# Who clears the Toeplitz table, and where four value tiles stand, in the state-space part of a two-block kernel

## The chip, the cores and the metric

The kernel runs on one core of a Trainium2 chip. The metric is the device time of one execution in microseconds. A core has TensorE (matmuls), VectorE, ScalarE, GpSimd, and SyncE, which here issues all DMAs. Each engine works through its own instructions in order and waits on semaphores. TensorE writes to PSUM, eight banks of 128 x 512 float32.

## The reference

Two transformer blocks over x of 1 x 1024 x 1024, all float32. The first block mixes a state-space part (S5) and retention, then a convolutional feed-forward; the second has three branches (differential attention, and two gated linear attentions), then a feed-forward. The change is in the first block's mixer:

```
h = x @ w_in                        # 1024 -> 512 (u), 256 (q), 256 (k), 512 (v), 512 (gate)
bu = einsum('blgc,gpc->blgp', u, b_bar)                   # 32 groups, 64 complex states
_, states = associative_scan(_ssm_combine, (a_elems, bu))
y = real(einsum('blgp,gcp->blgc', states, c)) + d * u
y = gelu(y);  y_s5 = rms_norm(y * sigmoid(y @ glu_w + glu_b))
y_ret = retention(rotary(q), rotary(k), v) * silu(gate)   # 16 chunks of 64, 4 heads
x = layer_norm(ALPHA * x + concat(y_s5, y_ret) @ w_out)
```

## The kernel before

Every float32 weight is cut in two parts, high and low, and each product is made of three matmuls (high x high, high x low, low x high). A weight unit of 128 x 1024 is loaded into one of three buffers WR, ScalarE writes its high part WH (L1167), GpSimd its low part WL (L2538), and there are five places for cut units. `act_cut(e, done)` and `pool_cut(e, done)` run up to five units ahead of `done`. Units 0 to 3 are the state-space input, 4 to 7 the queries and keys, 8 to 11 the values, 12 and 13 the weights of the gated linear unit (GLU).

The order of the work is written out by hand on each engine. The PSUM banks are handed out by a counter in the order of TensorE's program (`claim`), so an instruction moved there also moves the banks of what follows: a claim waits until the last user of its bank has been read.

**The state-space part** works in eight positions of a block at a time. With TensorE it computes: `kernel_of(p)`, four groups of the short convolution kernel (L548); `inject(q)`, eight groups that bring the input into the states (L537); `outputs(q)`, four groups of 32 T8 products (L561) with twice as many products of the states (L563). In its words a value tile is one step of `values` (`tick(values, n)`), 24 matmuls of 128 x 512 (L476 to L478) that make one of eight tiles of v. It has nothing to do with the state-space part and fills TensorE's time in it.

T8 is the Toeplitz table, 128 x 32 x 128, 16 KB on each partition. It is zero above its diagonal blocks. GpSimd adds the diagonal term to the four parts of the kernel (`through`, L2649), clears T8 (L2673), and SyncE, which waits for the clearing (`s_t8z`), writes the eight shifted copies of the kernel from memory into it (L2846). T8 lies over the tables from which the kernel was made, so it can be cleared only when these have been read (`s_et`, `s_kd`). `outputs(0)` waits for T8 (`t8_in`) and for the states of its group (`s_ss`).

VectorE turns each injected group by the phase table ET, scans it along the time and turns it back (`dve_s5`); it waits for `inject(q)` and frees that group's bank with the fifth of its instructions (L1910). After each second group it reports four more groups of states (`s_ss`).

ScalarE copies the value tiles from PSUM into the buffer STQ (L1198), from where SyncE spills them to memory, and applies gelu to the outputs (L1220, L1222), which needs another function table than the copies. Behind the state-space part comes retention: SyncE loads the spilled queries and keys back (QKC) when all states are done, GpSimd rotates them (L2626 to L2637), TensorE transposes them (`flip`, L502) and computes the scores (`scores`, L604), with value tiles 5, 6 and 7 in between. ScalarE copies the transposed chunks (KQT, L1172), and between two of them cuts the landed state-space output YP for the GLU (GH, L1335).

Of the kernel before, what the change touches and what calls it, by code (L numbers as in the profile page):

```python
# [10 lines left out]
ACT = mybir.ActivationFunctionType  # L11
# [238 lines left out]
def build(nc, D, out):  # L250
    plan, order1, order2 = weight_plan()
    with ExitStack() as ctx:
# [3 lines left out]
        def sem(name):  # L256
# [19 lines left out]
        s_pp, s_cl, s_bb, s_et, s_t8z, s_kd, s_ss = (sem(n) for n in (  # L276
            "s5_powers", "s5_c_powers", "s5_b_powers", "s5_tables_read", "s5_toeplitz_zero", "s5_kernel_done", "s5_states"))
# [40 lines left out]
        ones = sb("ones", 204.5, [128, 128])  # L318
# [38 lines left out]
        T8 = sb("T8", 132, [128, 32, 128])  # L357
# [57 lines left out]
        lots = bk.at  # L415
# [89 lines left out]
        def pe_mixer(e):  # L505
            prep = claim(e, "prep", 2, hold=True, told=False)
            for p in range(4):
                v = wt.next("w_in", 0, 8, 128 * p, 128)
                u = claim(e, ("u", p), 2)
# [64 lines left out]
            values = pe_token_steps(e, "v", "w_in", 1024, 0, 8, XH, XL, range(8))  # L574
# [9 lines left out]
            tick(values, 2)  # L584
            inject(4)
            inject(5)
            outputs(0)
            tick(values, 1)
            inject(6)
            inject(7)  # L590
            outputs(1)
            tick(values, 1)
            outputs(2)
            tick(values, 1)
            outputs(3)

            def scores(i):
# [304 lines left out]
        def tick(steps, n):  # L902
            for _ in range(n):
                next(steps, None)
# [296 lines left out]
        def act_s5(e):  # L1201
            def turned(q):
                act_evac(e, lots["bbt", q], BB[:, 2 * q:2 * q + 2, :, :].rearrange("p a b c -> p (a b c)"))

            def kernel_of(p):
                u = lots["kt", p]
                k = KTS[p % 2]
                if p == 1:
                    e.wait_ge(s_cl, 4)
                if p >= 2:  # L1210
                    e.wait_ge(kt_out[p % 2], 16)
                e.wait_ge(u.full, u.nfull)
                e.activation(k[:, 0:8:2, :], PS[0:16, u.b, :].rearrange("p (a c) -> p a c", a=4), ACT.Copy).then_inc(act, ca.up())
                e.activation(k[:, 1:8:2, :], PS[0:16, u.b + 1, :].rearrange("p (a c) -> p a c", a=4),
                             ACT.Copy).then_inc(u.drained, 1)

            def outputs(q):
                u = lots["y8", q]
                e.wait_ge(u.full, u.nfull)
                e.activation(U8[:, 8 * q:8 * q + 8:2, :], PS[:, u.b, :].rearrange("p (a c) -> p a c", a=4),  # L1220
                             ACT.Gelu_apprx_tanh).then_inc(act, ca.up())
                e.activation(U8[:, 8 * q + 1:8 * q + 8:2, :], PS[:, u.b + 1, :].rearrange("p (a c) -> p a c", a=4),  # L1222
                             ACT.Gelu_apprx_tanh).then_inc(u.drained, 1)

            def values(*blocks):
                for i in blocks:
                    act_spill(e, "v", i)

            for i in range(5):
                act_spill(e, "qk", i)  # L1230
            for q in range(4):
                turned(q)
            act_spill(e, "qk", 5)
            act_spill(e, "qk", 6)
            for q in range(4, 8):
                turned(q)
            act_spill(e, "qk", 7, 4)
            kernel_of(0)
            kernel_of(1)
            act_cut(e, 6)  # L1240
            kernel_of(2)
            kernel_of(3)
            act_cut(e, lots["qk", 7].units)
            values(0, 1)
            outputs(0)
            values(2)
            outputs(1)
            values(3)
            outputs(2)
            values(4)  # L1250
            outputs(3)

        def act_retention(e):
# [1387 lines left out]
        def pool_kernel(e):  # L2641
            idb = ident[0:16, 0:16].rearrange("p (o c) -> p o c", o=1).to_broadcast([16, 8, 16])
            e.wait_ge(dm_in, 16)
            e.wait_ge(cst, 32)

            def through(p):
                u, k = lots["kt", p], KTS[p % 2]
                e.wait_ge(u.drained, u.ndrained)
                e.tensor_tensor(k[:, :, 0:16], k[:, :, 0:16], diag(p), ALU.add).then_inc(s_kd, 1)  # L2649

            def diag(p):
                return sm[0:16, 128 * (p % 2):128 * (p % 2) + 128].rearrange("p (g c) -> p g c", c=16)

            def spread(p):
                if p >= 2:
                    e.wait_ge(s_kd, p - 1)
                e.tensor_tensor(diag(p), idb, DM[:, 8 * p:8 * p + 8].rearrange("p (g o) -> p g o", o=1).to_broadcast([16, 8, 16]),
                                ALU.mult).then_inc(pool, cg.up())
                e.wait_ge(pool, cg.n)

            spread(0)
            spread(1)
            through(0)
            through(1)
            spread(2)
            spread(3)
            pool_cut(e, 6)
            through(2)
            through(3)
            u = lots["kt", 3]  # L2670
            e.wait_ge(u.full, u.nfull)
            e.wait_ge(s_et, 1)
            e.memset(T8[:, :, :], 0.0).then_inc(s_t8z, 1)  # L2673
            pool_cut(e, lots["qk", 7].units)

        def cuts(cut, e, name):
# [526 lines left out]
```

## Time and profile before

| | us |
|---|---|
| median of three runs (3144.47 to 3147.0) | 3144.47 |
| the profiled execution | 3141.87 |
| its span, first to last instruction | 3139.6 |
| TensorE busy in it | 3041.6 (97%) |
| ScalarE, VectorE, GpSimd busy | 913.7, 1245.6, 1047.0 |

The granted TensorE clock is 0.991 of full speed in the mean over the span. The stretch of the change is 100 to 215 us; the kernel goes on for another 2900 us after it. A timeline row gives start, duration, engine, line, operation, written tile and read tiles, and in brackets the idle time before it and what ended it. Rows of several instructions are merged (x4). In the profile T8 is called T, U8 is U, and M1 to M3 are M.

### The profile page before, as it was taken

To read this page: it belongs to the slowest core of one execution; us is meant where nothing else is said; L and a number is where in the kernel's file an instruction comes from. 1 tells how busy PE (TensorE), PEld (TensorE's weight loads), DVE (VectorE), ACT (ScalarE), POOL (GpSimd) and SP (SyncE) were. 2 spreads that over 40 slices of the span, in tenths; PEclk is the share of its full clock that TensorE was granted. 3 is DMA by queue.
4 is the path that set the end of the run, shared out by engine and by line. 5 is a ranking of instruction groups with operands and counts; after the bars stand their busy time and mean duration, and the time that the engine had idled before them with its cause. 6 is when DMAs were issued, how large, how long until landed. Compare 5 with 4: busy or idle time off the path is not lost.

```text
span 3139.6 us, 35710 instructions
## 1 busy us (share of the span) xinstructions
PE 3041.6 (97%) x14710; PEld 2499.1 (80%) x14710; DVE 1245.6 (40%) x2353; ACT 913.7 (29%) x1340; POOL 1047.0 (33%) x514
## 2 busy tenths in 40 slices
PE   8999999999999999999999999999999999999998
PEld 7777788888888877777777777788888788888886
DVE  8837642112221155454536644532545111121115
ACT  3223342121211233333424543432333212111111
POOL 4443354322323252111322333232223733333335
PEclk9899999999999999999999999999999999999999
DMA  6332311111111112111110111124330111111111
GB/s 210 85 110 69 101 47 48 53 62 47 47 47 54 47 63 88 48 55 61 41 44 31 54 47 54 41 68 157 138 134 28 59 49 68 47 47 47 54 41 54
DMA packets 70897, 207.62 MB, mean 66 GB/s; under 512 B 11376, under 2 KB 19968, under 8 KB 70720
## 3 DMA queue, kind: packets, MB, share of 16 engines
q1 hardware_dynamic: 70736, 205.34, 20.4%
q8 instruction: 117, 1.92, 0.3%
q14 instruction: 44, 0.36, 0.0%
HBM read 172.54 MB, written 32.77 MB: 65 GB/s over the span
## 4 chain that ended last, share of the span: by engine, by line
PE 85%; POOL 4%; ACT 3%; DVE 3%; issue 3%; DMA 1%; SPq 0%; ACTq 0%; DVEq 0%; POOLq 0%
PE PS L436 48%; PE PS L476 7%; PE PS L478 7%; PE PS L477 7%; PE PS L756 3%; PE PS L1067 3%; POOL WL L2538 2%; PE PS L944 1%; PE PS L974 1%; PE PS L502 1%; PE PS L563 1%; PE PS L858 1%; PE PS L859 1%; PE PS L857 1%; PE PS L957 1%
## 5 line engine op out<-in xcount | busy, mean ns | idle before, releaser
L2538 POOL TENSOR_TENSOR WL<-WR,WH 128x1024 fp32r<-128x1024 f32 x241 | 580.5, 2416 | 1853.9 <-ACT WH L1167 1853.8
L436 PE MATMUL PS<-XH,WH 128*128 128x512 f32 x2176 | 690.8, 399 | 16.9 <-DVE XL L1788 9.2
L436 PE MATMUL PS<-XL,WH 128*128 128x512 f32 x2176 | 674.4, 391 | 0.0
L436 PE MATMUL PS<-XH,WL 128*128 128x512 f32 x2176 | 672.2, 390 | 0.0
L436 PEld LDWEIGHTS PS<-XH,WH 128*128 128x128 f32 x2176 | 397.1, 189 | 108.4 <-issue 25.4
L436 PEld LDWEIGHTS PS<-XL,WH 128*128 128x128 f32 x2176 | 410.1, 188 | 87.4
L436 PEld LDWEIGHTS PS<-XH,WL 128*128 128x128 f32 x2176 | 409.6, 188 | 87.7
L1167 ACT ACTIVATE WH<-WR 128x1024 fp32r<-128x1024 f32 x241 | 253.2, 1055 | 666.8 <-PE PS L478 443.3
L476 PE MATMUL PS<-WH,HH 128*128 128x512 f32 x736 | 286.4, 389 | 2.5 <-POOL HL L2570 2.5
L477 PE MATMUL PS<-WL,HH 128*128 128x512 f32 x736 | 286.3, 389 | 0.0
L478 PE MATMUL PS<-WH,HL 128*128 128x512 f32 x736 | 286.3, 389 | 0.0
L2167 DVE TENSOR_TENSOR CT<-CT,PS 128x1024 f32<-128x1024 f32 x54 | 65.9, 1221 | 459.1 <-ACT CT L1392 310.9
L2180 DVE TENSOR_TENSOR XF<-XF,PS 128x512 f32<-128x512 f32 x160 | 110.0, 687 | 313.2 <-PE PS L478 313.2
L476 PEld LDWEIGHTS PS<-WH,HH 128*128 128x128 f32 x736 | 138.1, 188 | 31.6 <-POOL HL L2570 2.9
L478 PEld LDWEIGHTS PS<-WH,HL 128*128 128x128 f32 x736 | 138.1, 188 | 28.7
L477 PEld LDWEIGHTS PS<-WL,HH 128*128 128x128 f32 x736 | 138.1, 188 | 28.7
L476 PE MATMUL PS<-WH,XH 128*128 128x512 f32 x384 | 153.7, 400 | 4.7 <-POOL WL L2538 3.0
L478 PE MATMUL PS<-WH,XL 128*128 128x512 f32 x384 | 151.4, 394 | 0.0
L477 PE MATMUL PS<-WL,XH 128*128 128x512 f32 x384 | 151.2, 394 | 0.0
L2570 POOL TENSOR_TENSOR HL<-CT,HH 128x1024 fp32r<-128x1024 f32 x54 | 129.5, 2399 | 7.6 <-ACT HH L1398 7.6
L2161 DVE SCALAR_TENSOR_TENSOR CT<-PS,cols,CT 128x1023 f32<-128x1023 f32 x22 | 28.2, 1283 | 238.3 <-ACT CT L1385 238.3
L2389 DVE COPY_PREDICATED ST<-LV,PS 128x512 f32<-128x512 uint8 x128 | 85.7, 726 | 70.0 <-PE PS L1067 69.8
(349 smaller groups left out, 3986.0 us busy)
## 6 DMA issues: line engine op xcount, KB each, us to landing
WR<-in_weights SPq DMA_DIRECT2D x241, 512.0 KB, 3.6
gates<-EG SPq DMA_DIRECT2D x18, 512.0 KB, 5.2
EI<-gates SPq DMA_DIRECT2D x18, 512.0 KB, 4.7
BR<-brbuf SPq DMA_DIRECT2D x12, 512.0 KB, 6.3
RAWX<-in_xT SPq DMA_DIRECT2D x8, 512.0 KB, 7.6
spill<-STQ SPq DMA_DIRECT2D x16, 256.0 KB, 2.3
RX<-in_x SPq DMA_DIRECT2D x8, 512.0 KB, 6.5
xbuf<-XF SPq DMA_DIRECT2D x8, 512.0 KB, 2.6
```

Source lines behind the costliest of these rows:

```text
L436: last = e.matmul(PS[:, u.b + h, :], w, x[:, k, 512 * h:512 * h + 512], start=k == 0 and w is w1 and x is xh, stop=k == nk - 1 and w is w2)
L476: e.matmul(PS[:, u.b, :], a, wh[:, k, :], start=j == 0 and k == 0, stop=False)
L477: e.matmul(PS[:, u.b, :], a, wl[:, k, :], start=False, stop=False)
L478: last = e.matmul(PS[:, u.b, :], c, wh[:, k, :], start=False, stop=j == len(vs) - 1 and k == 1)
L756: last = e.matmul(PS[:, u.b + h, :], w[:, k, :], x[:, k, 512 * h:512 * h + 512], start=k == 0 and w is wh and x is XH, stop=k == 7 and w i ...
L1067: last = e.matmul(PS[:, us[g][hh].b, 128 * (i % 4):128 * (i % 4) + 128], kl[rows[hh], c], kr[rows[hh], c], start=True, stop=True)
L1167: e.activation(WH[:, v % NSPL, :], WR[:, v % NRAW, :], ACT.Copy).then_inc(w_hi, 1)
L2167: e.tensor_tensor(X, X, bank(u, 2), ALU.mult).then_inc(u.drained, 1)
L2180: e.tensor_tensor(x, x, bank(u), ALU.add).then_inc(u.drained, 1)
L2389: e.copy_predicated(o, LV[:, n:n + 1, :].to_broadcast([128, 4, 128]), four(u)).then_inc(u.drained, 1)
L2538: e.tensor_tensor(WL[:, v % NSPL, :], WR[:, v % NRAW, :], WH[:, v % NSPL, :].bitcast(F), ALU.subtract).then_inc(w_lo, 1)
L2570: e.tensor_tensor(HL[:, v % 5, :], CT[:, v % 2, :], HH[:, v % 5, :].bitcast(F), ALU.subtract).then_inc(f_lo, 1)
```

## The change

Four edits, all of them in order alone; no arithmetic is added or removed:

- ScalarE clears T8, with a copy of the ones table scaled by 0, behind its cuts of units 11 and 12 and ahead of value tile 0. It waits for `s_et` and for all four kernel parts (`s_kd`).
- GpSimd no longer clears it, so that the low parts of units 11 and 12 stand right behind the last two kernel additions.
- On TensorE value tiles 2 and 3 stand ahead of `outputs(0)`; tile 4 stands behind `outputs(1)`. Before, tile 2 stood behind `outputs(0)`, tile 3 behind `outputs(1)`, tile 4 behind `outputs(2)`.
- ScalarE's copies follow: tiles 0 to 3, then the gelu of two output groups, tile 4, the gelu of the last two.

SyncE's program is the same: it still stores output group 0 ahead of value tile 2 and group 1 ahead of tile 3.

```diff
@@ pe_mixer @@
             inject(4)
             inject(5)
+            tick(values, 2)
             outputs(0)
-            tick(values, 1)
             inject(6)
             inject(7)
             outputs(1)
             tick(values, 1)
             outputs(2)
-            tick(values, 1)
             outputs(3)
@@ act_s5 @@
             act_cut(e, lots["qk", 7].units)
-            values(0, 1)
+            e.wait_ge(s_et, 1)
+            e.wait_ge(s_kd, 4)
+            e.activation(T8[:, :, :], ones[:, :].rearrange("p (o c) -> p o c", o=1).to_broadcast([128, 32, 128]), ACT.Copy,
+                         scale=0.0).then_inc(s_t8z, 1)
+            values(0, 1, 2, 3)
             outputs(0)
-            values(2)
             outputs(1)
-            values(3)
+            values(4)
             outputs(2)
-            values(4)
             outputs(3)
@@ pool_kernel @@
             through(3)
-            u = lots["kt", 3]
-            e.wait_ge(u.full, u.nfull)
-            e.wait_ge(s_et, 1)
-            e.memset(T8[:, :, :], 0.0).then_inc(s_t8z, 1)
             pool_cut(e, lots["qk", 7].units)
```

TensorE, from value tile 1's end to output group 1, before. L537 is an injected group, L561 an output group's first product, L476 the first matmul of a value tile; rows without a wait are left out.

```order
L537 MATMUL PS<-U_71,BB 64x128 [waits bank0_drained,bank4_drained]
...
L561 MATMUL PS<-U_71,T_116 128x128 [waits t8_landed,s5_states,bank2_drained]
...
L476 MATMUL PS<-WH,XH 128x512 [waits bank4_drained]
...
L537 MATMUL PS<-U_71,BB 64x128 [waits bank5_drained]
...
L537 MATMUL PS<-U_71,BB 64x128 [waits bank6_drained]
...
L561 MATMUL PS<-U_71,T_116 128x128 [waits s5_states,bank1_drained,bank0_drained]
```

The same place now:

```order
L537 MATMUL PS<-U_71,BB 64x128 [waits bank0_drained,bank4_drained]
...
L476 MATMUL PS<-WH,XH 128x512 [waits bank2_drained]
...
L561 MATMUL PS<-U_71,T_116 128x128 [waits s5_states,t8_landed,bank5_drained,bank4_drained]
...
L537 MATMUL PS<-U_71,BB 64x128 [waits bank6_drained,bank5_drained]
...
L537 MATMUL PS<-U_71,BB 64x128 [waits bank7_drained,bank6_drained]
...
L561 MATMUL PS<-U_71,T_116 128x128 [waits s5_states,bank1_drained,bank0_drained]
```

Two value tiles (each begins with a wait for bank 2 or a neighbour) have moved ahead of output group 0, and that group now takes banks 4 and 5, which were injected groups 2 and 3's, instead of 2 and 3.

GpSimd, from the last two kernel additions to the first rotated chunk, before:

```order
L2649 TENSOR_TENSOR KTS_107<-KTS_107,sm 16x8x16 [waits bank0_drained]
L2649 TENSOR_TENSOR KTS_108<-KTS_108,sm 16x8x16 [waits bank2_drained]
L2673 MEMSET T_116 128x4096 [waits s5_tables_read,bank2_full]
L2538 TENSOR_TENSOR WL<-WR,WH 128x1024 [waits weight_high_cut] x2
L2626 TENSOR_TENSOR TA_81<-QKC,RT 128x256 [waits ret_tables_landed,qk_chunk_landed0]
```

The same place now:

```order
L2650 TENSOR_TENSOR KTS_107<-KTS_107,sm 16x8x16 [waits bank0_drained]
L2650 TENSOR_TENSOR KTS_108<-KTS_108,sm 16x8x16 [waits bank2_drained]
L2539 TENSOR_TENSOR WL<-WR,WH 128x1024 [waits weight_high_cut] x2
L2627 TENSOR_TENSOR TA_81<-QKC,RT 128x256 [waits ret_tables_landed,qk_chunk_landed0]
```

The clearing is gone, and the two low parts have nothing ahead of them but the additions.

## Rows read from the trace of the kernel before

**Rows 1.** Chain of waits, 100 to 215 us: start us, us, what.
```profile
113.62 3.48 POOL T L2673
...
122.23 9.14 DMA T<-ktbuf
...
192.33 0.65 PE PS L563 x4
```

**Rows 2.** Windows, TensorE: stretch, us, busy (instructions), granted clock, DMA share, GB/s.
```profile
116.40:119.40 3.00, 0.32 (x2) 1.00 0.13 14
...
131.50:146.50 15.00, 14.99 (x49) 0.50 0.31 121
...
146.50:151.70 5.20, 5.20 (x13) 0.50 0.46 75
```

**Rows 3.** Timeline, TensorE: start us, us, line, operation [idle before, releaser].
```profile
119.44 0.50 PE L476 MATMUL PS<-WH,XH 128*128 128x512 f32 x1 [2.73 <-POOL WL L2538]
...
131.51 0.76 PE L561 MATMUL PS<-U,T 128*128 128x128 f32 x2 [3.07 <-DMA T<-ktbuf]
...
146.46 0.79 PE L476 MATMUL PS<-WH,XH 128*128 128x512 f32 x1
...
154.71 1.97 PE L537 MATMUL PS<-U,BB 128*64 128x128 f32 x32
...
156.60 0.49 PE L561 MATMUL PS<-U,T 128*128 128x128 f32 x2
...
165.06 0.50 PE L476 MATMUL PS<-WH,XH 128*128 128x512 f32 x1
...
170.63 0.38 PE L561 MATMUL PS<-U,T 128*128 128x128 f32 x2
```

**Rows 4.** Timeline, GpSimd (POOL), 85 to 262 us.
```profile
107.69 4.85 POOL L2538 TENSOR_TENSOR WL<-WR,WH 128x1024 fp32r<-128x1024 f32 x2
...
113.57 3.52 POOL L2673 MEMSET T<- 128x4096 f32 x1
...
117.06 4.67 POOL L2538 TENSOR_TENSOR WL<-WR,WH 128x1024 fp32r<-128x1024 f32 x2
...
176.72 0.72 POOL L2626 TENSOR_TENSOR TA<-QKC,RT 128x256 f32<-128x256 f32 x1 [54.99 <-DMA QKC<-spill]
...
186.47 0.61 POOL L2637 TENSOR_TENSOR KZ<-QKC,RT 128x256 f32<-128x256 f32 x1
```

**Rows 5.** Timeline, VectorE (DVE), 85 to 262 us.
```profile
108.18 2.15 DVE L1749 TENSOR_TENSOR BB<-M 128x256 f32<-128x256 f32 x1
...
110.36 4.01 DVE L1749 TENSOR_TENSOR_SCAN BB<-LAM,BB 128x128 f32<-128x128 f32 x4
...
115.26 0.42 DVE L1749 TENSOR_TENSOR BB<-M 128x256 f32<-128x256 f32 x1
...
116.51 5.51 DVE L1749 TENSOR_TENSOR BB<-M 128x256 f32<-128x256 f32 x1
...
122.05 1.80 DVE L1749 TENSOR_TENSOR_SCAN BB<-LAM,BB 128x128 f32<-128x128 f32 x4
...
147.56 0.42 DVE L1749 TENSOR_TENSOR BB<-M 128x256 f32<-128x256 f32 x1
...
155.90 0.42 DVE L1749 TENSOR_TENSOR M<-PS,ET 128x256 f32<-128x256 f32 x1 [1.87 <-PE PS L537]
...
168.14 0.69 DVE L1931 TENSOR_TENSOR BB<-M,M 128x508 f32<-128x508 f32 x1
```

**Rows 6.** Timeline, ScalarE (ACT), 85 to 262 us.
```profile
113.90 1.06 ACT L1167 ACTIVATE WH<-WR 128x1024 fp32r<-128x1024 f32 x1 [1.26 <-DMA WR<-in_weights]
...
121.19 0.60 ACT L1198 ACTIVATE STQ<-PS 128x512 f32<-128x512 f32 x1 [6.23 <-PE PS L478]
...
204.95 1.06 ACT L1335 ACTIVATE GH<-YP 128x1024 fp32r<-128x1024 f32 x1 [1.05 <-DMA YP<-ybuf]
...
205.92 0.58 ACT L1172 ACTIVATE KQT<-PS 128x512 f32<-128x512 f32 x1
```

## Prediction

> **What bounds the kernel now.** I read the busy line first: TensorE is busy 97% of the span, so only its idle time and its clock can give anything. Then I followed the chain of waits through the stretch that the diff touches, 100 to 215 us. It goes: GpSimd's last kernel addition, the clearing of T8 (3.48 us from 113.62), eight Toeplitz loads, the landing of the last of them after 9.14 us at 131.37, and from there only TensorE's own work until the last output group ends at 192.98 [rows 1]. The reader is to see that the chain runs through the clearing, not through TensorE's work before 131.37: two value tiles and the state matmuls end at 128.44 and then TensorE waits 3.07 us [rows 3].
>
> The granted clock is the second thing to see. It is 1.00 (the 2.4 GHz level) in the wait at 116.4 and 0.50 (1.2 GHz) from 131.5 to 151.7, right behind the second wait [rows 2]. Output group 0 takes 14.95 us there (131.51 to 146.46), group 1 at the full clock 8.46 (156.60 to 165.06). Value tile 2 takes 8.25 (146.46 to 154.71), tile 3 at the full clock 5.57 (165.06 to 170.63) [rows 3]. So the wait of 3.07 costs 9.2 us more in slow matmuls than it lasts itself.
>
> A third, smaller loss: value tile 0 stands 2.73 us for the low part of weight unit 11, which GpSimd makes only behind the clearing, at 117.06 [rows 3, 4].
>
> **The change, part by part.** Times are those of the trace of before, moved.
>
> Clearing on ScalarE. Its last cut before the value tiles ends at 114.96 [rows 6]. Its copies take 0.60 us for 512 columns and 1.06 for 1024 [rows 6], 0.9 ns a column, so 4096 columns cost some 3.8 us (bounds: 3.5, as GpSimd's clearing, and 7.6, twice the price of a column, which no plain copy in the rows comes near). The table is clear at 118.8 instead of 117.10, and SyncE's eight loads, the two weight loads and the tables behind them go out 1.7 us later. T8 lands at 133.1 instead of 131.37. Behind the clearing on ScalarE stand the copies of value tiles 0 to 3; tile 0 ends near 117.8, so its copy waits 1 us, on no path, since the PSUM bank is not wanted again soon. Even the upper bound lands T8 at 136.9.
>
> Two value tiles before output group 0. By the sum below TensorE comes to group 0 at 139.2. T8 is there 6 us before that. The 3.07 us are gone, and with them the only idle time that stood ahead of the fall of the clock: gain 3.07 + (14.95 - 8.46) + (8.25 - 5.57) = 3.07 + 6.49 + 2.68 = **12.2 us**. Value tile 4 moves to between groups 1 and 2: no work added or removed.
>
> GpSimd's low parts follow each other. Unit 11's can start at 113.6 and end near 116.0, before tile 0 wants it at 116.4: the 2.73 us are gone at that place. But what is late next? Tile 1 goes to bank 7, which VectorE frees when it has read state group 1 out of PSUM. Before, it had done so at 116.47 (the instruction ahead of the one at 116.51), in the shadow of the clearing, and its instructions with two SBUF inputs ran at full pace in that time (0.42 us at 115.26) [rows 5]. Beside low parts they don't: the subtraction at 108.18 took 2.15 us and the four scans 4.01 instead of 1.80 while GpSimd made two low parts from 107.69, and the subtraction at 116.51 took 5.51, until the pair from 117.06 was through at 121.73 [rows 4, 5]. Now the pair runs 113.6 to 118.4 and falls on the fourth scan. If VectorE slips in between the two parts (as at 110.33), group 1 is read by 120.2; if not (as at 116.51), by 121.0. Before, tile 1 began at 119.44 plus a quarter of a tile, 120.8. So this part gives between +0.6 and -0.2; I take **0.2 us**, not 2.7.
>
> The Trainium skill, page "SBUF — State Buffer", section "Who interferes with whom", says that a VectorE instruction with two SBUF inputs and a GpSimd instruction that reads SBUF exclude each other for the whole instruction; a clearing reads nothing. By that rule the moved low parts do hit the scan, and the edit's own gain is the 0.2 above; without it tile 1 would begin at 117.8 and the sum would be 15. The trace agrees (0.42 against 5.51 us).
>
> VectorE from there: its next scans began at 122.05; now at 120.7 to 121.5, so its chain runs 0.5 to 1.4 us earlier, and its wait of 1.87 us for state group 6 goes too, since TensorE does that group at 147.7. Its last states come at 168.83 - 1 - 1.87 = 166.0 [rows 5].
>
> The banks move with the tiles. Output group 0 now takes the banks of state groups 2 and 3, group 1 those of 4 and 5. Group 5 was read just ahead of the instruction at 147.56 [rows 5], now by 147; output group 1 starts at 149.6. That is a margin of over 2 us and costs nothing.
>
> Sum for TensorE: tile 1 from 120.6 to 126.05; state groups 4, 5 to 128.2; tiles 2, 3 to 139.2; output 0 to 147.7; states 6, 7 to 149.6; output 1 to 158.1; tile 4 to 163.6; outputs 2 and 3 to 180.5. Before: 192.98. That is **12.4 us**.
>
> Retention's start. The rotated keys need VectorE's last states (166.0) and then the load. GpSimd began on them at 176.72, 7.9 us after the states, and was through with two chunks at 187.08 [rows 4]. In front of that load SyncE stores output group 1 and a value tile; group 1 ends at 158.1 now, and the stores are gone by 163 (an estimate), so the states set the load, the keys begin between 171 and 174 and two chunks are done by 181 to 184. The first transpose needs one chunk at 180.5, the second both, more than 6 us later. New waits: scores 0 takes the bank of tile 5 and stands for its copy (0.60 us), tile 6 stands for the masking of scores 0, tile 7 for the copy of the second transposed chunk. That copy ended at 206.50, 13.5 us after the last output group, since it stands in ScalarE's queue behind the landing of YP's last quarter [rows 6]; tile 7 is wanted two tiles (11.1) and an estimated 2.5 us of small work and the two waits after it, 13.6. Against that tile 5 no longer stands for a copy. I take 0, between -1 and +1. Behind that the free banks are those of two places earlier throughout, which changes who waits for whom only around two of the six gated jobs: under 1 us either way.
>
> **Sum: 12.4 us, taken as 12.5.** The profiled execution took 3141.87 us (span 3139.6), so 3129.4 on its basis; it is the fastest of those shown. On the median, 3144.47, it is **3132.0**.
>
> **Rivals.**
> - No collision on VectorE. For it: a scan's second input is one column repeated. Against: the scans at 110.36. Tile 1 starts 2.8 us earlier: 15.3 us, 3129.2. 10%.
> - The clock halves once anyway. TensorE still stands 2.4 to 3.2 us before tile 1 and has the thin matmuls of the states before and behind. Against: the wait of 2.73 at the same place left the clock at 1.00 [rows 2]. Same price as before, 9.2 us: gain 3.3, 3141.2, which a measurement can't tell from no change (I take 0.2%, 6.3 us, as what it can tell). 11%.
> - Retention takes it back: tile 7 stands for the chunk's copy. The margin is nil, and YP's landing waits in SyncE's queue behind sixteen small stores and three loads. Each us late is lost; with 4 us 3136.0. 9%.
> - Slower. The clock halves at the wait before tile 1 and stays there past the 20.2 us that it lasted before. A tile costs 4.9 us more then (12 in 5.2 us at the half clock, beside the one begun before [rows 2], so 24 in 10.4), so tiles 1 to 3 eat 14.7 us, more than the gain: from the third tile on it is a loss. With output group 0 (6.5) it is 21.2 - 12.5 = 8.7 slower, 3153.2. Against it: a busy TensorE had its clock back after 20 us. 4%.
>
> **How the numbers follow.** Forecast 66%, rivals 10, 11, 9 and 4. The forecast's own range is 3129.5 to 3134.5 (bounds of the collision and of retention's start). From 3126.5 (first rival, and a run as much below the median as the profiled one) to 3141.5 (second rival) all but the slow case and some tails are inside. Faster by over 0.2%: the forecast, the first rival and most of the third, 84%. Within 0.2%: 12%. Slower: 4%.
>
> **What would show it.** Granted clock 1.00 from 120 to 180; no wait of TensorE for T8; output group 0 in 8.5 us beginning near 139; a wait of some 2.4 to 3.2 us before value tile 1 where there was one of 2.73 inside tile 0; a scan of VectorE stretched over GpSimd's pair; ScalarE's clearing 3.5 to 4.2 us; the last output group's end near 180.5; tile 7 without a long wait. It is wrong if a stretch of 0.50 stands behind 120, if output group 0 still ends with T8's landing, or if the 12 us at 180 are no longer there at 215.

## The result, and the profile after

The changed kernel takes 3133.36 us in the median of six executions (3127.94 to 3136.61), the kernel before 3144.47 of six (3140.63 to 3147.0). The ratio is 0.9966, with a 95% interval of 0.9955 to 0.9976: 11.1 us faster. Nine more executions, measured later beside fourteen of the kernel before, gave a median of 3135.7 against 3144.11, ratio 0.9976 (0.9967 to 0.9986): 8.4 us faster. The profiled execution took 3131.03 us, its span is 3129.2 at a mean granted clock of 0.994 (before: 3139.6 at 0.991). Three executions of all that follow (one of before, 3419 us; one each of two experiments, 7861 and 9967 us) were slow as a whole and are left out.

Places are compared from one landmark on: GpSimd's last two kernel additions, at 112.51 us before and at 113.78 after, because the two spans don't begin alike. Line numbers of after are one more or one less than before.

TensorE's timeline, after, answers to [rows 3] (start, duration, engine, line, operation, written tile and read tiles; in brackets the idle time before it and what ended it):

```profile
122.86 0.50 PE L476 MATMUL PS<-WH,XH 128*128 128x512 f32 x1 [3.52 <-DVE M L1911]
...
130.12 1.97 PE L537 MATMUL PS<-U,BB 128*64 128x128 f32 x32
132.01 0.50 PE L476 MATMUL PS<-WH,XH 128*128 128x512 f32 x1
...
143.03 0.38 PE L561 MATMUL PS<-U,T 128*128 128x128 f32 x2
...
151.37 1.97 PE L537 MATMUL PS<-U,BB 128*64 128x128 f32 x32
184.14 0.66 PE L502 MATMUL PS<-ident,QKC 128*128 128x128 f32 x4
...
191.12 0.71 PE L603 MATMUL PS<-KQT 64*128 64x128 f32 x8 [0.84 <-ACT STQ L1197]
192.68 0.50 PE L476 MATMUL PS<-WH,XH 128*128 128x512 f32 x1 [0.26 <-DVE PT L1952]
...
214.52 0.70 PE L436 MATMUL PS<-GH,WH 128*128 128x512 f32 x2 [1.30 <-ACT SG L1260]
```

The wait for T8 is gone. Output group 0 runs from 143.03 to 151.37, 8.3 us instead of 14.95; tiles 2 and 3 together take the 11.0 us from 132.01. Tile 0 no longer stops, but tile 1 now begins with a wait of 3.52 us, for the bank that VectorE reads.

The windows view of TensorE, after, answers to [rows 2] (window, length, busy time and matmuls, granted clock, DMA share, GB/s):

```profile
119.40:122.80 3.40, 0.00 (x0) 1.00 0.24 33
122.90:124.10 1.20, 1.20 (x5) 1.00 0.96 170
124.20:127.40 3.20, 3.20 (x9) 0.50 1.32 121
127.80:130.10 2.30, 2.30 (x11) 1.00 1.87 189
132.10:143.00 10.90, 10.90 (x48) 1.00 0.56 200
```

After the wait the clock is at its full 2.4 GHz for 1.3 us, then at 1.2 GHz for 3.4 us, and then full again. Tile 1 takes 7.26 us (122.86 to 130.12); in the kernel before it took 5.54 (120.93 to 126.47). That is 1.7 us lost; the long stretch of before, 20 us from 131.5, does not come.

GpSimd, VectorE and ScalarE after, from their timelines, answer to [rows 4], [rows 5] and [rows 6]:

```profile
108.95 4.85 POOL L2539 TENSOR_TENSOR WL<-WR,WH 128x1024 fp32r<-128x1024 f32 x2
113.78 0.98 POOL L2650 TENSOR_TENSOR KTS<-KTS,sm 16x128 f32<-16x128 f32 x2
114.73 4.76 POOL L2539 TENSOR_TENSOR WL<-WR,WH 128x1024 fp32r<-128x1024 f32 x2
```

```profile
109.44 2.14 DVE L1750 TENSOR_TENSOR BB<-M 128x256 f32<-128x256 f32 x1
111.61 9.08 DVE L1750 TENSOR_TENSOR_SCAN BB<-LAM,BB 128x128 f32<-128x128 f32 x4
...
122.39 0.41 DVE L1911 TENSOR_TENSOR M<-PS,ET 128x256 f32<-128x256 f32 x1
```

```profile
115.83 3.61 ACT L1245 ACTIVATE T<-ones 128x4096 f32<-128x4096 f32 x1
```

GpSimd's four low parts now stand almost without a gap, and VectorE's four scans, 4.01 us before, take 9.08 behind them. The tile view of the scans (least, median and longest in ns, first and last start) and two windows of VectorE (length, its busy time and instructions) part them:

```profile
L1750 DVE TENSOR_TENSOR_SCAN BB<-LAM,BB x4: 424/1452/5648, 111.6 to 120.3; 128x128 f32<-128x128 f32 x4
```

```profile
111.60:114.10 2.50, 2.48 (x1) 1.00 0.60 187
114.10:119.50 5.40, 5.37 (x1) 1.00 0.42 135
```

The first scan takes 2.5 us. The second takes 5.65, until 119.78, and the second pair of low parts is through at 119.49; the other two pass at full pace. The kernel before had the same first scan, and then, with the clearing in place of the second pair, three quick ones (VectorE's timeline of before in narrow windows; x2 are two scans in one row):

```profile
110.36 2.47 DVE L1749 TENSOR_TENSOR_SCAN BB<-LAM,BB 128x128 f32<-128x128 f32 x1
112.86 1.04 DVE L1749 TENSOR_TENSOR_SCAN BB<-LAM,BB 128x128 f32<-128x128 f32 x2
113.94 0.42 DVE L1749 TENSOR_TENSOR_SCAN BB<-LAM,BB 128x128 f32<-128x128 f32 x1
```

So the first pair of low parts costs VectorE the same in both kernels, and the second pair alone makes the difference. State group 1 is therefore read out only at 122.80 (the last row of VectorE, 122.39 and its 0.41), and TensorE goes on at 122.86.

At the first GLU product that waits for ScalarE's sigmoid (7 us behind the first of all) the changed kernel is 10.3 us ahead: 214.52 less 113.78 is 100.74; before it is 111.02, by these two rows of its timelines:

```profile
112.51 1.11 POOL L2649 TENSOR_TENSOR KTS<-KTS,sm 16x128 f32<-16x128 f32 x2
```

```profile
223.53 0.70 PE L436 MATMUL PS<-GH,WH 128*128 128x512 f32 x2 [1.30 <-ACT SG L1259]
```

### The profile page after: what moved, and what is told of

Read it like the earlier page. It is cut to its first block, busy times and chain, and to the rows that moved or that the text cites. A ratio compares the mean times of both kernels' runs of the same rounds, so it can differ in the third digit from the quotient of the medians.

```text
span 3129.2 us, 35710 instructions
## 1 busy us (share of the span) xinstructions
PE 3033.6 (97%) x14710; PEld 2493.5 (80%) x14710; DVE 1245.5 (40%) x2353; ACT 917.1 (29%) x1341; POOL 1043.4 (33%) x513
## 3 DMA queue, kind: packets, MB, share of 16 engines
q1 hardware_dynamic: 70736, 205.34, 20.5%
## 4 chain that ended last, share of the span: by engine, by line
PE 86%; DVE 4%; POOL 3%; ACT 3%; issue 3%; DMA 0%; SPq 0%; ACTq 0%; DVEq 0%; POOLq 0%
PE PS L436 48%; PE PS L476 7%; PE PS L478 7%; PE PS L477 7%; PE PS L755 3%; PE PS L1066 3%; POOL WL L2539 2%; PE PS L943 1%; PE PS L973 1%; PE PS L502 1%; PE PS L858 1%; PE PS L857 1%; PE PS L856 1%; PE PS L563 1%; PE PS L956 1%
## 5 line engine op out<-in xcount | busy, mean ns | idle before, releaser
L476 PE MATMUL PS<-WH,HH 128*128 128x512 f32 x736 | 286.4, 389 | 2.5 <-POOL HL L2571 2.5
L476 PEld LDWEIGHTS PS<-WH,HH 128*128 128x128 f32 x736 | 138.1, 188 | 31.6 <-POOL HL L2571 2.9
L476 PE MATMUL PS<-WH,XH 128*128 128x512 f32 x384 | 153.3, 399 | 4.7 <-DVE M L1911 3.5
```

What stands on the lines that cost most here:

```text
L476: e.matmul(PS[:, u.b, :], a, wh[:, k, :], start=j == 0 and k == 0, stop=False)
```

## The measure used for the experiments

Three numbers stand for each kernel. The time and its ratio say what is gained. **The path** is the time from the last two kernel additions to that GLU product, in the profiled execution. **The span at full clock** is the span times its mean granted clock, averaged over all executions; what is left of the span is what the half clock took. The span at full clock is known to about 0.3 to 0.7 us where the time of one execution moves by 10, since it is the clock that differs from one execution to the next. It has three weak points. The clock is given to three digits, a step of 3.1 us, so it means something only as an average over several executions. And it counts half of each slow stretch as lost, while the matmuls here lose a little less: of the 20.2 us at half clock before it counts 10.1, the rows of output group 0 and tile 2 show 9.2. And it counts the end of the span, where TensorE has nothing left to do: 3.5 us in the traces of before and of the changed kernel alike.

| kernel | executions | span at full clock | taken by the clock | path | half clock in the path |
|---|---|---|---|---|---|
| before | 48 | 3110.2 | 30.6 | 111.0 | 20.5 us |
| changed | 15 | 3109.2 | 23.0 | 100.7, 100.8 | 3.4 us in both |
| tiles' order alone | 12 | 3108.1 | 23.2 | 98.6, 98.4 | none in both |
| clearing alone | 12 | 3110.8 | 29.6 | 104.8, 109.5 | 6.8 us; 17.1 us |
| changed, tile 1's own bank | 13 | 3105.3 | 27.5 | 96.3, 102.3 | none; 13.7 us |
| changed, unit 12 later | 5 | 3105.7 | 23.2 | 96.9 | none |
| put together | 5 | 3104.0 | 24.4 | 94.6 | none |
| tile 1's bank and tile 4 earlier | 5 | 3105.4 | 21.9 | 95.3 | none |
| put together and tile 4 earlier | 5 | 3102.0 | 23.1 | 93.9 | none |

The means of the two clock columns are uncertain by 0.5 to 1.3 us where there are ten executions or more and by about 2 where there are five. Two paths or stretches in a cell are two profiled executions of one kernel.

The first line against the second is the result again: of the 8.6 us of mean span that the change saves, 7.6 come from the clock and 1.0 from everything else. The kernels were measured at different times and in part on different chips, each beside the kernel before, whose mean at full clock was 3110.4, 3110.2 and 3110.0 there.

## Experiments: each part of the change alone

**The tiles' order alone**, GpSimd clearing as before:

```diff
@@ pe_mixer, from the kernel before @@
             inject(5)
+            tick(values, 2)
             outputs(0)
-            tick(values, 1)
...
@@ act_s5 @@
-            values(0, 1)
+            values(0, 1, 2, 3)
...
```

> One part of the change alone: the kernel before, with value tiles 2 and 3 ahead of output group 0 and tile 4 behind group 1 on TensorE and ScalarE; GpSimd clears T8 as before. My theory (the whole gain comes from the tiles' new order, and the clearing's move only trades one small loss for another): no wait for T8, output group 0 in 8.5 us at the full clock, tile 0 again with a stop of some 2.7 us for its low part, no wait of more than 0.5 us before tile 1, granted clock 1.00 from 120 to 180. The 12.2 us come whole, so about 3132 against 3144.5 before, and 0 to 2.5 us faster than the changed kernel. Rival (the move of the clearing is needed, since T8 or the low parts are late without it): 3135 or more, with a stop at T8 or at a low part over 3 us. Second rival (any stop of TensorE near 117 to 123 is followed by a fall of the clock): a stretch of 0.50 of 3 us or more behind tile 0's stop, as in the changed kernel, and about the changed kernel's time, 3133.

Measured: 3135.07 us, ratio 0.9971 (0.9959 to 0.9983), 3 us over the 3132 expected and not faster than the changed kernel's 3133.36. There is no usable trace of it, so two more measurements follow, the second beside the changed kernel:

> A second profiled execution of the kernel with the tiles' order alone, to see its trace. Theory: tile 0 stops some 2.7 us for its low part, no stop over 0.5 us before tile 1, no wait for T8, and no fall of the clock between 110 and 200; the first scores begin within 2 us of the changed kernel's place, counted from the last two kernel additions. Rival (the clearing on GpSimd is then on the path): a stop for T8, or for a low part, of over 3 us.

> The tiles' order alone, again, beside the changed kernel on one chip, since its first five times (3130.0 to 3136.7) don't part it from the changed kernel and its one good trace is 2.1 us ahead of it at 215 us (1.7 of that the changed kernel's short fall of the clock). Theory (the moved clearing is worth nothing, or less): median 0 to 2.5 us under the changed kernel's of the same call. Rival (the moved clearing gains): median 1 us or more above it.

Measured: 3128.76 us for the one execution of the second measurement; in the third 3132.99 us, ratio 0.9969 (0.9957 to 0.9980), beside 3135.7 and 0.9976 (0.9967 to 0.9986) for the changed kernel. Timelines (TensorE, VectorE, GpSimd) of the second measurement's execution:

```profile
119.57 0.50 PE L476 MATMUL PS<-WH,XH 128*128 128x512 f32 x1 [2.71 <-POOL WL L2535]
```

```profile
110.49 4.01 DVE L1746 TENSOR_TENSOR_SCAN BB<-LAM,BB 128x128 f32<-128x128 f32 x4
...
116.64 5.51 DVE L1746 TENSOR_TENSOR BB<-M 128x256 f32<-128x256 f32 x1
```

```profile
113.70 3.52 POOL L2670 MEMSET T<- 128x4096 f32 x1
117.19 4.68 POOL L2535 TENSOR_TENSOR WL<-WR,WH 128x1024 fp32r<-128x1024 f32 x2
```

Tile 0 stops for its low part as before (2.71 us), tile 1 goes straight on, and no fall of the clock follows. The path is 2.1 to 2.4 us shorter than the changed kernel's and 12.4 to 12.7 shorter than before. The theory of the waits holds, and both rivals fall: the stop of 2.71 brings no fall of the clock, and no stop at T8 is left. The moved clearing is worth nothing. The third measurement's medians are even 2.7 us apart in favour of the order alone (0 to 2.5 was expected), but the intervals overlap.

**The clearing alone**, with the value tiles in the old order:

```diff
@@ pe_mixer, from the changed kernel @@
             inject(5)
-            tick(values, 2)
             outputs(0)
+            tick(values, 1)
...
@@ act_s5 @@
-            values(0, 1, 2, 3)
+            values(0, 1)
...
```

> The other part alone: the changed kernel with the value tiles of before in their old places; ScalarE clears T8 and GpSimd's low parts follow each other. My theory: T8 lands later than before (131.4) by the later clearing, 1.7 us or more, TensorE reaches output group 0 as early as before, so it waits 3 to 6 us for T8, and the stretch at 0.50 behind that wait is there as before (output group 0 near 15 us). Time 3144 to 3149, no gain and possibly 1 to 4 us slower than before. Rival (the clearing's move is what gains): 3140 or less, a shorter wait for T8 than 3.07 us.

Measured: 3140.93 us in eleven executions (3135.4 to 3150.5), ratio 0.9997 (0.9986 to 1.0008). No gain, as expected; the range for the time was set 3 us too high. But the wait for T8 was only 1.91 us, and no fall of the clock came behind it. I had expected 3 to 6. T8 does land later: output group 0 begins 20.2 us behind the landmark (133.48 less 113.26), before 19.0 (131.51 less 112.51). What I had left out is that TensorE is late too, held before tile 1 and slowed in it. The 6.8 us of half clock in this path are 3.4 in tile 1 and 3.4 behind a wait of 1.08 us at 187.50. The profiled execution was the fastest of the eleven, so a second one was profiled:

> A second profiled execution of the kernel with the clearing alone; the first was its fastest of eleven (3135.4; median 3140.9) and had no fall of the clock behind the wait for T8. Theory (that fall does not follow a wait in each execution, only in most): this one has a stretch of 0.50 of some 10 to 20 us behind the wait for T8, and a time of 3139 to 3148. Rival (the shorter wait for T8, 1.91 us, doesn't bring the fall; the time lies elsewhere): clock 1.00 from 131 to 175 again, and the difference to 3135.4 in stretches of 0.50 in other places.

Measured: 3145.27 us. The first matmul of output group 0 in the first and in the second execution, from TensorE's timeline:

```profile
133.48 0.46 PE L561 MATMUL PS<-U,T 128*128 128x128 f32 x2 [1.91 <-DMA T<-ktbuf]
```

```profile
133.79 0.46 PE L561 MATMUL PS<-U,T 128*128 128x128 f32 x2 [2.21 <-DMA T<-ktbuf]
```

Windows of TensorE in the second:

```profile
134.00:136.00 2.00, 2.00 (x13) 1.00 1.05 424
136.00:140.00 4.00, 4.00 (x15) 0.58 0.56 217
140.00:146.00 6.00, 6.00 (x21) 0.50 0.00 0
```

From 110 us to state groups 4 and 5 at 129.61 the two executions agree in every row of TensorE to 0.05 us. Then one waits 1.91 us and keeps its clock, the other waits 2.21 us and has 13.7 us of half clock. The theory holds: the fall follows the wait in some executions and not in others. What the length of the wait has to do with it can't be told from two.

## Experiments: what holds tile 1

**Another bank for tile 1.** Tile 1 took bank 7 by the counter, where state group 1 lies. The list gives the banks of the eight value tiles (None is the counter's), and `bk.turn` sets the counter:

```diff
@@ pe_mixer, from the changed kernel @@
-            values = pe_token_steps(e, "v", "w_in", 1024, 0, 8, XH, XL, range(8))
+            values = pe_token_steps(e, "v", "w_in", 1024, 0, 8, XH, XL, range(8), (6, 2, 3, 7, None, None, None, None))
...
             tick(values, 2)
+            bk.turn = 0
             inject(4)
             inject(5)
             tick(values, 2)
+            bk.turn = 4
             outputs(0)
```

> The changed kernel with one difference, the banks of value tiles 0 to 3: 6, 2, 3, 7 in place of the counter's, so that tile 1 does not stand on the bank that state group 1 still fills, and the counter set so that all behind them keep theirs. GpSimd's pair and VectorE's held scan stay. My theory (the wait of 3.52 us before tile 1 comes from that bank and the clock's short fall from that wait): no wait over 0.5 us before tile 1, granted clock 1.00 from 120 on, tile 1 in 5.45 us in place of 7.26, last output group's end 5.3 us earlier, time about 3128 against 3133.4. State groups 4 and 5 want the banks of 0 and 1 next and may wait 0 to 1.5 us for VectorE, so 3128 to 3130. Rival (VectorE's chain is the bound there, and the wait only moves to state group 4 or to output group 0): 3132 to 3134, with a wait of 3 us or more in a new place. Second rival (the clock's fall has another cause than the wait): 3130, with a stretch of 0.50 still near 124.

Measured: 3136.8 us, ratio 0.9974 (0.9963 to 0.9984), with the twelve executions in two groups (five of 3128.5 to 3130.7, seven of 3136.4 to 3140.1). The place is as the theory has it: VectorE's scans still take 9.09 us, TensorE doesn't wait before tile 1, the clock stays full there, and the path is 4.4 us shorter. One wait is new, 0.98 us before output group 1. The profile names no releaser for it ("issue"). It ends at 147.61, and VectorE's reading of state group 5, whose bank that group takes, ends at 147.51:

```profile
147.61 0.46 PE L561 MATMUL PS<-U,T 128*128 128x128 f32 x2 [0.98 <-issue]
```

```profile
147.10 0.41 DVE L1913 TENSOR_TENSOR M<-PS,ET 128x256 f32<-128x256 f32 x1
```

But the time, where the theory had 3128 to 3130, is no better than the changed kernel's. So a second execution was profiled:

> A second profiled execution of the kernel with tile 1's own bank, whose twelve times fell into five of 3128.5 to 3130.7 and seven of 3136.4 to 3140.1, at mean clocks of 0.992 to 0.993 and 0.990 to 0.991. Theory (the stretch of the change is the same in every execution and the clock falls in other places, more or fewer of them): again no wait before tile 1 and the same times up to 215 us within 0.3 us; if the time is one of the long ones, the difference of 6 to 10 us lies wholly in stretches of 0.50 behind 215 us. Rival (the long executions have a wait or a fall of the clock in the stretch of the change): a wait of over 1 us or a stretch of 0.50 between 105 and 215 us.

Measured: 3131.41 us. TensorE's timeline at output group 1, and the windows behind it:

```profile
148.98 0.46 PE L561 MATMUL PS<-U,T 128*128 128x128 f32 x2 [0.96 <-issue]
```

```profile
144.00:147.00 3.00, 3.00 (x31) 1.00 0.00 0
...
149.00:151.00 2.00, 2.00 (x12) 1.00 0.82 140
151.00:153.00 2.00, 2.00 (x9) 0.61 0.81 204
153.00:155.00 2.00, 2.00 (x8) 0.50 0.59 183
155.00:160.00 5.00, 5.00 (x18) 0.50 0.09 35
```

This execution has the same wait (0.96 against 0.98) and then 13.7 us of half clock, which the other didn't have; its path is 6.0 us longer. So the rival was right in part: the clock can fall in the stretch of the change. Yet this is not one of the long executions (its time is 3131.4), since it lost less behind 215 us. Both things part the executions.

**The low part of unit 12 later**, the same bank as in the changed kernel:

```diff
@@ pool_kernel, from the changed kernel @@
             through(3)
+            pool_cut(e, 7)
+            u = lots["inj", 1]
+            e.wait_ge(u.drained, u.ndrained)
             pool_cut(e, lots["qk", 7].units)
```

> The changed kernel with one difference on GpSimd: it makes the low part of unit 11 at once, but that of unit 12 only when VectorE has read state group 1 out of its bank. My theory (the two low parts one behind the other hold VectorE's scan for 5.66 us, and so tile 1's bank): the scan is held by one low part only, 2 to 3.5 us, the wait before tile 1 is 0.5 to 1.5 us in place of 3.52, no fall of the clock near 124, time 3129 to 3131 against 3133.4. Tile 1 to 3 need only unit 11 and below, so the later unit 12 costs nothing. Rival (VectorE is late for another reason than GpSimd's second part): the wait stays 3 us or more, and the time within 1 us of the changed kernel's.

Measured: 3131.57 us, ratio 0.9960 (0.9948 to 0.9972). From its VectorE, GpSimd and TensorE timelines:

```profile
110.88 6.71 DVE L1750 TENSOR_TENSOR_SCAN BB<-LAM,BB 128x128 f32<-128x128 f32 x4
...
120.20 3.88 DVE L1750 TENSOR_TENSOR_SCAN BB<-LAM,BB 128x128 f32<-128x128 f32 x4
```

```profile
114.00 2.39 POOL L2539 TENSOR_TENSOR WL<-WR,WH 128x1024 fp32r<-128x1024 f32 x1
119.78 2.64 POOL L2539 TENSOR_TENSOR WL<-WR,WH 128x1024 fp32r<-128x1024 f32 x1 [3.39 <-DVE M L1911]
```

```profile
119.76 0.50 PE L476 MATMUL PS<-WH,XH 128*128 128x512 f32 x1 [1.16 <-DVE M L1911]
```

With one part less behind the scans they take 6.71 us instead of 9.08, and the wait before tile 1 is 1.16 us instead of 3.52: 2.37 and 2.36 less, the length of one part (2.39). No fall of the clock follows. The theory holds for the scans (the caught one takes 3.28 us, 2 to 3.5 expected), the wait and the clock; the time is 0.6 us over the range. The collision of GpSimd's low parts with VectorE's scans is the cause of the wait.

## Experiments: put together, and the next wait

The put-together kernel has both edits above, and value tiles 5, 6 and 7 in banks 5, 3 and 7, so that the scores and tile 6 stand for nobody (the line that differs from both; the rest of both edits is as above):

```diff
@@ pe_mixer, from the changed kernel @@
-            values = pe_token_steps(e, "v", "w_in", 1024, 0, 8, XH, XL, range(8), (6, 2, 3, 7, None, None, None, None))
+            values = pe_token_steps(e, "v", "w_in", 1024, 0, 8, XH, XL, range(8), (6, 2, 3, 7, None, 5, 3, 7))
```

> Put together: the changed kernel with tile 1 and its neighbours in their own banks, value tiles 5, 6 and 7 in banks 5, 3 and 7 so that the scores and tile 6 stand for no copy, and GpSimd's part of unit 12 behind the reading of state group 1. Theory: no wait of TensorE over 0.3 us from the first value tile to the second transposed chunk, so 5.3 us (tile 1) and 1.1 us (retention) less than the changed kernel, and the wait of 0.98 us ahead of output group 1, which the bank change alone showed, gone with VectorE's scan held by one part only. Counted without the clock's falls that is 6.4 us less than the changed kernel (1.3 to 2 less than with the bank alone); the time by the mean of the falls in the kernels so far 3127 to 3132 against 3133.4 and 3144.3. Rival (more falls of the clock behind the stretch eat what is won in it, as the bank change's long executions suggest): 3133 or more with a clock of 0.990 or 0.991 in most executions.

Measured: 3128.38 us, ratio 0.9963 (0.9949 to 0.9977); at full clock 5.2 us less than the changed kernel, where 6.4 was expected. The waits of 0.84 and 0.26 us in retention are gone. The wait before output group 1 is not: VectorE comes earlier, but so does TensorE, and 0.69 us stay. That step of the theory failed. Of five executions two were long (3133.3 and 3136.7, clocks of 0.991 and 0.990), so the rival was partly right too.

The last two kernels give VectorE time there, with value tile 4 ahead of output group 1 instead of behind it, on TensorE and on ScalarE, once in the put-together kernel and once in the kernel with tile 1's own bank:

```diff
@@ pe_mixer, from either @@
             inject(7)
+            tick(values, 1)
             outputs(1)
-            tick(values, 1)
             outputs(2)
@@ act_s5 @@
             outputs(0)
-            outputs(1)
             values(4)
+            outputs(1)
             outputs(2)
```

> The put-together kernel with value tile 4 moved ahead of output group 1 on TensorE and ScalarE (it stood behind it), so that VectorE has 5.5 us more to read state group 5 out of the bank that output group 1 takes. Theory (the wait of 0.69 to 0.98 us before output group 1 is for that bank, and a long fall of the clock follows it in part of the executions): no wait over 0.3 us before output group 1, 0.7 us less than the put-together kernel without the clock's falls (some 3103.3 us of span), no stretch of 0.50 between 105 and 215 us, and the executions closer together: 3124 to 3131, median 3127. Rival (the falls that part the executions lie behind 215 us): again two or more of five executions at a clock of 0.991 or less and over 3132.

> The kernel with tile 1's own bank alone, with tile 4 ahead of output group 1 as well. It had a wait of 0.96 to 0.98 us before output group 1, and seven of twelve executions at 3136 to 3140; one profiled execution had 13.7 us of half clock right behind that wait. Theory (the wait and its fall part the executions): the wait is gone and no more than one of the executions is over 3134; median 3128 to 3131. Rival (the fall comes of itself or in another place): the same two groups, about half of the executions over 3136.

Measured: the first 3127.85 us, ratio 0.9949 (0.9935 to 0.9962); the second 3130.38 us, ratio 0.9957 (0.9945 to 0.9969). In the first TensorE's only wait between 100 and 215 us is the GLU's, by its waits view (engine and line, what they waited for: us in total, times, longest):

```profile
PE PS L436 <- ACT SG L1262: 1.3, 1, 1.3
```

The changed kernel has four there, 3.52, 0.84, 0.26 and 1.30 us (its rows stand at the result).

The first kernel's five executions lie between 3122.0 and 3129.5, the second's between 3124.8 and 3132.4. With the wait of 0.98 us gone, no execution is in the group over 3136 in which seven of twelve were. If the edit did nothing, all seven long ones of the seventeen executions would fall among the twelve about once in 25 times. That makes the wait and its fall of the clock a likely cause of the group, not a shown one: the two kernels were measured at different times on different chips, and the changed kernel itself had two groups the first time (three of 3127.9 to 3131.1, three of 3135.6 to 3136.6) and one the second (nine of 3133.1 to 3136.2). **The first is the fastest kernel of this study**: 16.3 us under before in the medians, and its interval ends (0.9962) below that of the changed kernel measured beside it (0.9967 to 0.9986).

**The changed kernel again**, as the measure beside these two:

> The changed kernel again, beside the other three on one chip, as their measure, and for a second trace of it. Theory: again a wait of 3.52 us before tile 1; the times 3128 to 3137 as before, and the differences between executions in stretches of 0.50, not in waits, so that span less half of these stretches is the same within 1 us (3109.7). Rival (a wait changes from one execution to the next): a row of the stretch of the change that differs by over 0.5 us.

Measured: 3135.7 us (3133.1 to 3136.2). From its timeline:

```profile
122.68 0.50 PE L476 MATMUL PS<-WH,XH 128*128 128x512 f32 x1 [3.53 <-DVE M L1911]
```

The wait is the same to 0.01 us and the path to 0.1. This profiled execution's span is 4.8 us longer than the first one's (3134.0 against 3129.2). The mean granted clock from 1100 to 1500 us shows what kind of difference that is. The windows view of three other executions: the first trace of the changed kernel, tile 1's own bank (first trace), and the bank with tile 4 earlier:

```profile
1100.00:1500.00 400.00, 385.37 (x1909) 0.99 0.18 60
```

```profile
1100.00:1500.00 400.00, 385.40 (x1889) 0.98 0.19 61
```

```profile
1100.00:1500.00 400.00, 385.36 (x1914) 1.00 0.19 63
```

No edit touches this part of the program, TensorE is busy for the same 385.4 us, and still the half clock takes 4 us of it in one, 8 in another and hardly any in the third (0.01 of 400 us is 4). The changed kernel's second trace has 0.98 there, 4 us more lost than its first, which is most of the 4.8. It is also how the kernel with tile 1's own bank can be 4.4 us ahead of the changed kernel at the GLU, counted from the landmark, and 0.3 behind at the end of the span, counted likewise (3015.7 against 3015.4).

## Why the prediction was right, point by point

The time, 3132.0, was met to 1.4 us (3133.36), the range and the direction too. That it came so near is in part luck: the later nine executions have 3135.7, which is outside the forecast's own range (3129.5 to 3134.5), and the gain there was 8.4 us. By the steps of the working:

- **The wait for T8 and the half clock behind it, 12.2 us: right.** 3.07 of wait, 6.6 of output group 0 (14.95 to 8.34) and 2.7 of tile 2 (8.25 to 5.5) make 12.4. The tiles' order alone shows it without admixture, 12.4 and 12.7 us of path. In the mean over all executions the clock took 7.6 us less; by the same measure the traces give 8.5 (20.5 less 3.4 us of half clock, halved), so the long stretch comes in most executions of the kernel before, if not in all. In a single execution it need not, since the fall can stay out (clearing alone, first trace).
- **Tile 1, +0.2 us: the term that was mis-sized.** That the low parts would fall on the scans and that tile 1 would wait for the bank was right, and so, nearly, was the expected wait, 2.4 to 3.2 us against 3.52. But the working let the pair fall "on the fourth scan". It caught the second (5.65 us), so that two more scans stood behind it. The rows of before, split up, have the second, third and fourth scan begin 0.35, 0.90 and 1.43 us behind the landmark, and the second pair's first row begins 0.95 behind it; even by these the third was next. State group 1 was read out at 122.80, where the later of the two expected times, 121.0, would be 122.3 on this trace's clock (its landmark is 1.27 us later). Counted from the landmark tile 1 started 0.7 us later than before (9.08 against 8.42) instead of 0.2 earlier, and ended 2.4 later (16.34 against 13.96).
- **The clock at that wait, second rival: it came, in small.** The rival's price was 9.2 us by the long stretch of before. It was 3.4 us of half clock and cost 1.7. All four traces with a wait of 3.52 us there have it. With the wait the fall goes, in the kernels with a bank of its own and with the later unit 12. The argument against the rival, that the wait of 2.73 had left the clock alone, was right for 2.73 (2.71 in the tiles' order alone) and didn't carry to 3.52.
- **Clearing on ScalarE: right.** 3.61 us against 3.8 expected, T8 1.2 us later (clearing alone) against 1.7, on no path.
- **Rule of the Trainium skill** (page "SBUF — State Buffer", section "Who interferes with whom"): the rule held for scans with one input repeated as well, so the first rival (no collision) falls. The scans' 9.08, 6.71, 4.01 and 1.80 us beside more and fewer low parts show it.
- **Retention, 0 ± 1 us: right.** Its first scores wait 0.84 us and tile 6 0.26, the copy's wait of 1.08 is gone; the changed kernel is 10.1 us ahead where the last output group ends (184.14 less 113.78 is 70.4, 192.98 less 112.51 is 80.5) and 10.3 at the GLU.
- **The banks of output groups 0 and 1, margin of over 2 us: right for this kernel, and narrow.** When TensorE came 4 to 5 us earlier the margin was gone, and a wait of 0.98 us took its place.

The terms add up in the traces. The long stretch gave 12.5 us (from state groups 4 and 5 to the last output group 66.51 before, 54.02 after), tile 1 took 2.4 back, which leaves the 10.1; the forecast had 12.4. The time of the profiled executions fell by 10.8 us (3141.87 to 3131.03): 10.3 in the path and 1.4 behind it, where the clock has eight falls of 3.4 us instead of nine, less the 1.3 by which its landmark stands later, and 0.4 outside the span. The forecast's picture of a clock at 1.00 from 120 to 180 was wrong: one of its own signs of being wrong, a stretch of 0.50 behind 120, did come.

## What to carry to other kernels

Before you lay a moved instruction beside another engine's work, split that engine's merged row into its single instructions: "x4, 4.01 us" hid where each scan began, and which one is caught decides how much stands behind it. Where the clock reacts to stops of TensorE, take a few executions' spans times their granted clocks: averaged over the executions, that number showed edits of 1 to 4 us that the times hid. A wait of TensorE of one to four microseconds can cost more by the fall of the clock behind it than by its length (3.07 us of wait and 9.2 of slow matmuls before). And when one engine gets earlier, the one that was just in time becomes the next one late.

## What the runs showed of the hardware that was not expected

- Four scans of 128x128, alone, take 1.80 us. Beside one low part of GpSimd's they take 3.88; beside the end of a first pair 4.01, with one more part behind it 6.71, with two more 9.08. A VectorE instruction that is caught between two low parts back to back gets in behind the first in some cases (the subtraction of 2.14 us) and in others not before both are through (5.51 and 5.65 us). The two that were held through both began, by their rows, 0.55 and 0.60 us before the pair, and alone take 0.42; why they did not get through first, no run here shows.
- The same kernel with the same wait keeps its clock in one execution and has 13.7 us of half clock in the next (tile 1's own bank): behind a wait of 0.98 us the clock stayed, behind one of 0.96 it fell. TensorE's rows before the wait agree to 0.02 us in the two. Likewise a wait of 2.07 us before a later product of the GLU has 3.4 us of half clock behind it in the trace of before (it ends at 273.75) and none in the changed kernel's (264.77).
- Executions of one kernel differ by up to 17 us in time (before, 3132.0 to 3148.8) while span times clock stays within 5. In the kernel before the clock takes 30.6 us in the mean. In its trace the stretch of the change has 10 us of that; the rest lies behind 215 us, where this study changed nothing: nine falls of 3.4 us, eight behind waits of 1.9 to 2.4 us and one behind two short ones (1.2 and 0.9), and the last 7 us, in which TensorE is idle.
